# A hybrid RWKV-7 / RetNet / HGRN2 backbone on one core: the order around RWKV's score products, and who writes a token mixing's own part

## What is computed

```python
def nbr_mean_seq(p):                      # context: mean of the two neighbours in the sequence
    pp = jnp.pad(p, ((0, 0), (1, 1), (0, 0)))
    return 0.5 * (pp[:, :-2] + pp[:, 2:])

def nbr_mean_grid(p):                     # latents: mean of the four neighbours in the grid
    ...
    m = 0.25 * (g[:, :-2, 1:-1] + g[:, 2:, 1:-1] + g[:, 1:-1, :-2] + g[:, 1:-1, 2:])

def rwkv7_mixer(p, h, v_first, vres, n_ctx, mu, ...):
    shifted = jnp.concatenate([nbr_mean_seq(p[:, :n_ctx]), nbr_mean_grid(p[:, n_ctx:])], axis=1)
    p = p + mu * (shifted - p)
    r, k, v, wd_f, wd_b, ad_f, ad_b, gd = split_sizes(p, RWKV_SIZES)
    if vres is None:
        v_first = v
    else:
        v = v + (v_first - v) * jax.nn.sigmoid(v0 + (h @ v_down) @ v_up)
    ...
    # a scan over the tokens in both directions with the state
    # S = S * exp(lw) - (S kk) (a * kk)^T + v k^T,  o = S r
    bonus = (jnp.sum(r_h * dirs[0][2] * r_k_h, axis=-1, keepdims=True)
             + jnp.sum(r_h * dirs[1][2] * r_k_h, axis=-1, keepdims=True)) * v_h
```

## Time and profile before

| what | value |
|---|---|
| time, median of 3 runs | 2741.78 us (2738.88 to 3275.7) |
| the profiled execution | 2744.85 us, of it 2743.1 us from the first to the last instruction |
| busy: TensorE matmuls | 2462.0 us (90%) |
| busy: TensorE weight loads | 1856.9 us (68%) |
| busy: VectorE | 1178.4 us (43%) |
| busy: ScalarE | 923.2 us (34%) |
| busy: GpSimd | 437.1 us (16%) |
| mean granted TensorE clock | 0.943 of full speed |
| RWKV groups, layer 0 | about 249 to 760 us, 127 us each |
| RWKV groups, layer 1 | about 1777 to 2228 us, 113 us each |

### The profile page before, as it was taken

One profiled execution on the slowest core, in us unless ns is written; L12 is line 12 of the kernel. 1 busy time (PEld: TensorE's weight loads), 2 busy tenths in 40 slices (PEclk: granted clock), 3 DMA queues, 4 the chain that ended last, 5 costly groups with the idle time before them and its releaser, 6 DMA issues.

```text
span 2743.1 us, 54656 instructions
## 1 busy us (share of the span) xinstructions
PE 2462.0 (90%) x23538; PEld 1856.9 (68%) x23538; DVE 1178.4 (43%) x1831; ACT 923.2 (34%) x1308; POOL 437.1 (16%) x455
## 2 busy tenths in 40 slices
PE   4988989898999889998999989888879898898998
PEld 1553748494855568876888856466857766598998
DVE  2323444444423343445444433254453523366665
ACT  3323232223234332334223342332232334345554
POOL 0002221212123310001000000132231314400000
PEclk8999999899999989998999989999989999899999
DMA  7313322313011023332233232200000012055553
GB/s 277 126 51 117 133 73 77 115 35 147 3 62 54 35 85 96 100 123 70 92 97 95 92 125 77 71 18 25 3 24 10 18 44 73 35 177 196 157 179 103
DMA packets 64031, 239.38 MB, mean 87 GB/s; under 512 B 7088, under 2 KB 8240, under 8 KB 62512
## 3 DMA queue, kind: packets, MB, share of 16 engines
q1 hardware_dynamic: 61920, 218.13, 24.0%
q10 hardware_dynamic: 1872, 17.75, 1.6%
HBM read 230.62 MB, written 5.24 MB: 86 GB/s over the span
## 4 chain that ended last, share of the span: by engine, by line
PE 79%; DVE 8%; ACT 6%; POOL 3%; issue 2%; DMA 2%; ACTq 0%; DVEq 0%; SPq 0%; POOLq 0%
PE psum L411 13%; PE psum L384 11%; PE psum L386 11%; PE psum L385 11%; PE psum L398 10%; PE psum L758 7%; PE psum L420 2%; PE psum L762 2%; PE psum L483 2%; PE psum L720 2%; PE psum L658 1%; POOL work L1799 1%; ACT L1383 1%; PE psum L447 1%; DMA work<-in_ret_constants 1%
## 5 line engine op out<-in xcount | busy, mean ns | idle before, releaser
L398 PE MATMUL psum<-normed,weight_ring 128*128 128x512 f32 (+1 forms) x864 | 372.5, 589 | 33.4 <-ACT normed L1437 12.6
L398 PEld LDWEIGHTS psum<-normed,weight_ring 128*128 128x128 f32 x864 | 176.5, 209 | 225.8 <-issue 210.2
L411 PE MATMUL psum<-work 64*64 64x64 f32 (+1 forms) x9088 | 307.7, 222 | 14.9 <-ACT work L1618 10.5
L929 DVE TENSOR_TENSOR weight_ring_parts<-weight_ring,weights_high 128x1024 fp32r<-128x1024 f32 (+1 forms) x224 | 266.7, 1191 | 125.5 <-ACT weights_high L1398 121.1
L411 PEld LDWEIGHTS psum<-work 64*64 64x64 f32 x9088 | 294.7, 135 | 26.6 <-issue 15.6
L385 PE MATMUL psum<-normed_low_part,weights_high 128*128 128x512 f32 (+1 forms) x896 | 304.1, 339 | 0.0
L1398 ACT ACTIVATE weights_high<-weight_ring 128x1024 fp32r<-128x1024 f32 (+1 forms) x224 | 230.8, 1030 | 160.5 <-PE psum L386 149.0
L758 PE MATMUL psum<-normed,weight_ring 128*128 128x512 f32 (+1 forms) x512 | 200.6, 539 | 2.7 <-ACT work L1383 2.7
L384 PE MATMUL psum<-normed_high,weights_high 128*128 128x512 f32 (+1 forms) x512 | 178.3, 348 | 15.6 <-DVE normed_low_part L917 15.2
L385 PEld LDWEIGHTS psum<-normed_low_part,weights_high 128*128 128x128 f32 x896 | 173.3, 193 | 21.3 <-issue 0.5
L386 PE MATMUL psum<-normed_high,weight_ring_parts 128*128 128x512 f32 (+1 forms) x512 | 176.9, 346 | 0.0
(11 more groups left out here) (241 smaller groups left out, 4218.6 us busy)
## 6 DMA issues: line engine op xcount, KB each, us to landing
weight_ring<-in_weights SPq DMA_DIRECT2D x406, 512.0 KB, 3.6
x_scratch<-work ACTq DMA_DIRECT2D x2, 2048.0 KB, 7.4
weight_ring<-in_weights SPq DMA_DIRECT2D x16, 256.0 KB, 2.8
work<-x_scratch ACTq DMA_DIRECT2D x2, 2048.0 KB, 10.3
work<-in_ret_constants ACTq DMA_DIRECT2D x2, 1152.0 KB, 12.7
work<-in_small_weights ACTq DMA_DIRECT2D x2, 1152.0 KB, 5.2
work<-in_x ACTq DMA_DIRECT2D x1, 2048.0 KB, 14.8
constants<-in_constants ACTq DMA_DIRECT2D x1, 1315.0 KB, 9.1
```

Source lines behind the costliest of these rows:

```text
L398: last = mm(ps[:, 0:t1 - t0], tiled(s, k), hT[:, k, t0:t1], start=(k == 0), stop=(k == KT - 1))
L411: last = mm(ps[q, w * m:w * m + w], lhs(q, m), rhs(q, m), start=True, stop=True)
L929: tt(ring_r[:, i % RING, o], ring[:, i % RING, o], high[:, n % HIGHS, o].bitcast(F32), ALU.subtract).then_inc(vec_split.sem, vec_split.ste ...
```

## The change

Five things are done.

1. **Order of the values.** On VectorE, mixing v (now a function `values`, in layer 1 with the difference to the first layer's values) moves from ahead of the first draining of gb to behind the draining of gk of direction 0. The first level of direction 0 moves behind the draining of gb of direction 1, and the gate products (`values_gated`) behind that. On ScalarE the gate's sigmoid moves from ahead of all transposes to between direction 0's and direction 1's.
2. **Bonus.** The two bonus products become one operation, and stand behind level j = 2.
3. **Own part.** ScalarE writes (1 - mu) x of all tokens straight from PSUM into the mixing's target, as a third operation of `raw`. The bank is free only after it. VectorE's two operations for that are gone.
4. **Neighbours.** GpSimd adds only the two vertical neighbours of the grid. VectorE adds the two horizontal ones into a new scratch (`sides`), as soon as the raw copy is there, and adds both parts in separate operations, so it has three operations for the latents and one for the context.
5. **The left-over column** of the prepared keys is made by a product with one, not by a copy.

TensorE's rows are the same as before.

```diff
 def mix(i, dst, key):
-    eng.wait_ge(pool_rwkv.sem, pool_rwkv.at("neighbours", l, i))
+    eng.wait_ge(act_rwkv.sem, act_rwkv.at("raw", l, i))
...
-    if ctx:
-        ts(dst[:, 0:NC], wk(raw + 1, NC), dcol(D_OMU + i), None, ALU.mult)
-    ts(dg, grid, dcol(D_OMU + i), None, ALU.mult)
+    tt(sides.rearrange("p (r t) -> p r t", t=GRID), grid[:, 1:5, 0:64], grid[:, 1:5, 2:66], ALU.add)
+    eng.wait_ge(act_rwkv.sem, act_rwkv.at("own part", l, i))
+    stt(dst[:, NC:N], sides, dcol(D_QMU + i), dst[:, NC:N], ALU.mult, ALU.add)
+    eng.wait_ge(pool_rwkv.sem, pool_rwkv.at("neighbours", l, i))
     if ctx:
         stt(dst[:, 0:NC], wk(raw + 654, NC), dcol(D_HMU + i), dst[:, 0:NC], ALU.mult, ALU.add)
     stt(dst[:, NC:N], wk(raw + 654 + NC, NC), dcol(D_QMU + i), dst[:, NC:N], ALU.mult, ALU.add)
...
-    cp(KR3[:, :, e:e + 1], kk3[:, :, e:e + 1])
+    tt(KR3[:, :, e:e + 1], kk3[:, :, e:e + 1], over_chunks(kcol(K_ONE, 1), 1), ALU.mult)
...
-    mix(8 + c, vv, ("mixed", l, 8 + c))
...
-    ts(ks, ks, pcol(l, "rk", c), None, ALU.mult)
-    tt(ks, ks, r[:, lo:N], ALU.mult)
...
     for d in range(2):
...
+        if d == 1:
+            first_level(0)
+            if l > 0:
+                values_gated()
         eng.wait_ge(wide_filled.sem, wide_filled.at("gk", l, c, d))
...
-        tt(chunks(B + BT), chunks(B + LT), over_chunks(kcol(K_LEV, 64), 64), ALU.mult)
-        tt(chunks(B + RR), ident64(kc), chunks(B + BT), ALU.subtract)
+        if d == 0:
+            values()
+    first_level(1)
...
+        if j == 2:
+            stt(ks, ks, pcol(l, "rk", c), r[:, lo:N], ALU.mult, ALU.mult)
...
 def raw(i, dst, ps, key):
...
     act(grid, latent, ACT.Copy)
+    act(dst[:, t0:N], ps[:, 0:N - t0], ACT.Copy, scale=dcol(D_OMU + i))
...
 def neighbours(i):
...
     tt(s3, grid[:, 0:4, 1:65], grid[:, 2:6, 1:65], ALU.add)
-    tt(s3, s3, grid[:, 1:5, 0:64], ALU.add)
-    tt(s3, s3, grid[:, 1:5, 2:66], ALU.add)
```

More of the change, by code:

```diff
@@ L1538, in _ @@
                     eng.wait_ge(big_filled.sem, big_filled.at("small", l, j))
-                    raw(12 + j, big.get("small", l, j), ("drained", "small", l, j))
+                    raw(12 + j, wk(RW_SMALL + 512 * j), big.get("small", l, j), ("drained", "small", l, j))
                 if l > 0:
@@ L1585, in _ @@
                     project(2)
-                    if l > 0:
-                        eng.wait_ge(vec_rwkv.sem, vec_rwkv.at("mixed", l, 8 + c))
-                        eng.wait_ge(big_filled.sem, big_filled.at("vgate", l, c))
-                        act(wk(RW_SCR), big.get("vgate", l, c), ACT.Sigmoid, bias=pcol(l, "v0", c)).then_inc(act_rwkv.sem, act_rwkv.step(("drained", "vgate", l, c)))
-                        eng.wait_ge(act_rwkv.sem, act_rwkv.n)
-                        act_rwkv.also(("vgate sigmoid", l, c))
                     modulation("kk", l, c)
@@ L1596, in _ @@
                         for n, dst in (("tkk", chunks(B + YK, 64, 64, 128)), ("tb", chunks(B + BTT)), ("tk", chunks(B + KTT))):
+                            if l > 0 and d == 1 and n == "tkk":
+                                eng.wait_ge(vec_rwkv.sem, vec_rwkv.at("mixed", l, 8 + c))
+                                eng.wait_ge(big_filled.sem, big_filled.at("vgate", l, c))
+                                act(wk(RW_SCR), big.get("vgate", l, c), ACT.Sigmoid, bias=pcol(l, "v0", c)).then_inc(act_rwkv.sem, act_rwkv.step(("drained", "vgate", l, c)))
+                                eng.wait_ge(act_rwkv.sem, act_rwkv.n)
+                                act_rwkv.also(("vgate sigmoid", l, c))
                             eng.wait_ge(mid_filled.sem, mid_filled.at(n, l, c, d))
```

62 lines of the change are left out of this document (33 added, 29 removed).

## The result

| | before | changed |
|---|---|---|
| time, median | 2741.35 us (4 runs) | 2691.69 us (4 runs, 2690.81 to 2699.12) |
| ratio of the times | 1 | 0.9828, 95% interval 0.9805 to 0.9851 |
| span of the profiled execution | 2743.1 us | 2689.1 us |
| mean granted TensorE clock | 0.943 | 0.956 |
| busy: TensorE, VectorE, ScalarE, GpSimd | 2462.0, 1178.4, 923.2, 437.1 us | 2439.7, 1187.7, 942.7, 406.5 us |

The forecast was 2701 us; the changed kernel is 1.7% faster. The medians there were 2701.79 and 2705.62 us, with ratios of 0.9842 (0.9818 to 0.9866) and 0.9865 (0.9841 to 0.9889); one further execution, of 9735 us, is as far outside as the 3275.7 us of the first table and is left out.

A forecast was written before the change was run, and what follows sets the result against it. TensorE's matmuls were taken as the bound (79% of the chain). Layer 1's 39.5 us (4 x 9.5 + 1.5) and layer 0's 1.6 gave 41 us less: 2701 us, own bounds 2690 to 2714, widened by rivals to 2684 to 2722.

The forecast's parts named there:

- The bound, and the wait to go: TensorE's matmuls bound the kernel; in layer 1 its 31.7 us of waiting for L1170, gb's draining, would go.
- Start of a group: Layer 1, up to gb: value projection starts as before, keys are prepared earlier, gb starts 2.0 us earlier.
- From gb on: Layer 1, step by step from gb's start to the level product of direction 1, the stretch's end: 17.7 us.
- The size a group: Layer 1: stretch ends at 1931.2 instead of 1940.75, 9.5 us less in each of four groups.
- The 1.5 us expected for the first group alone: Layer 1, first group only: gain at the value projection's wait for ScalarE's draining, 2.5 us there before.
- Work costed at nothing: Sigmoid ahead of direction 1's transposes (2 us if uncovered), bonus product (0.7 if uncovered), 8-column product: each counted as zero.
- Layer 0: Layer 0: 5.3 gained from L973's wait, 2.5 ahead of groups, 4.2 lost to ScalarE, 2 to clock: 1.6 us.
- Ahead of the groups: Layer 0, wait of 3.91 us for mixing, table load and sigmoid: shorter by 1.5 plus 1.0, 2.5 us.
- A (VectorE stays the bound): Layer 1: values' mixing overlaps GpSimd's sums at up to 1.4 us; only 4.3 us a group, 2722 us; chance 0.15.
- B (the clock in layer 0): Layer 0: shorter waits keep the clock up, 3 us back in each group; 2682 us; chance 0.13.
- C (the clock falls more): All eight groups: ScalarE's third operation lengthens two waits and slows the clock, 6.9 us a group; 2750 us; chance 0.04.
- D (the values' transpose takes over the wait): Layer 1: transposing the values waits for the gate as gb did, nothing moves; 2742 us; chance 0.05.

The follow-up runs named there:

- gate_first: The changed kernel with VectorE's gate products ahead of the first level of direction 0, not behind it; 2691.04 us, ratio 0.9817.
- sigmoid_first: The changed kernel with ScalarE's gate sigmoid put back ahead of all transposes, not only those of direction 1; 2725.0 us, ratio 0.994.
- bonus_split: The changed kernel with the bonus product in its new place but as two VectorE operations again; 2695.81 us.
- order_only: The kernel before with the new VectorE and ScalarE order and the one-operation bonus inside a level, but the old mixing; 2708.35 us, ratio 0.987.
- after_again: The changed kernel unaltered, run again on another chip as yardstick; 2701.79 us, ratio 0.9842.
- after_third: The changed kernel unaltered, run again beside another later set of experiments; 2705.62 us, ratio 0.9865.
- bonus_back: The changed kernel with the two old bonus operations back at their place behind preparing the keys; 2702.61 us.
- copy_back: The changed kernel with the 8-column product made a copy again; 2695.58 us, ratio 0.982.
- own_back: The changed kernel with VectorE writing the own part again, the sum of two neighbours staying on VectorE; 2698.08 us, ratio 0.9834.

## Why the prediction was right, point by point

**The bound, and the wait to go.** Right. L1170's wait is gone but for 1.7 us, and layer 1's groups gave 42.3 us; the sum had 39.5. The prediction calls the product behind the 7.60 us gb of direction 1; it is gk of direction 0, as said above. In its own sum for the change it has the order right, so no term is wrong by it. The 0.3 us left there were to stand ahead of gb of direction 1, and 0.47 do.

**Start of a group.** L1551, ScalarE's third operation, takes 0.69 us for 128x512 as costed. The line that ends the key preparation starts 5.98 us behind the value projection. The forecast had 5.5 to 6.7 (1910.3 to 1911.5 against 1904.8), and VectorE met GpSimd's L1812 with one operation of r's mixing (1.38 us) and with the one behind it (1.37 us). gb starts 8.61 us behind the value projection, for 10.72 before: a gain of 2.1, where the sum took 2.0.

**From gb on.** The working put the end of the stretch 17.7 us behind gb; it is 17.31. The steps in between hold too: gb of direction 1 at 6.17 (6.1), gk of direction 1 behind a wait of 0.42 (0.7), the collision of a gate product with GpSimd (0.95 us more), and the transposing of the values at 13.86 (14.4). `gate_first` shows the collision's price net of what follows it: 0.75 us a group, less than the 1.3 the working had given, since the next wait in line takes back 0.84.

**The size a group.** 9.5 us were forecast for the stretch and 9.99 measured. The second group's interval shrank by 10.1 us, so nearly all of it lies in the stretch; the three intervals shrank by 10.5 on average. Of the 9.99 us, 2.8 are the clock. The 1.5 us expected for the first group alone hardly show in this execution, in which its interval shrank by 10.9 us against 10.1 and 10.4. In the kernel's other two profiled executions that interval is 99.1 and 99.2 us, 13.5 us shorter than before. The difference is the clock: the matmuls of this interval were busy for 91.95 us here, at a granted clock of 0.95, and for 87.43 us in both others, at 1.00. The first group's low-rank products had the same wait of 0.61 us for ScalarE in all three, so that wait alone does not decide it.

**Work costed at nothing.** The transposes' banks behind the sigmoid: right as the change has it. The prediction put 2 us on losing that cover, the duration of table load and sigmoid. No run takes the cover away at that place. `sigmoid_first`, which leaves the sigmoid ahead of direction 0's transposes, costs 6.0 us of waiting a group, since the sigmoid also waits until the values are mixed. So the duration alone is no measure of what a lost cover costs. The bonus product: right (`bonus_split`). The 8-column product: right, no gain. For it the prediction had cited a page of the Trainium skill (SBUF — State Buffer, "Who interferes with whom"), by which a VectorE instruction with both inputs in SBUF waits for a GpSimd instruction that reads SBUF. The trace of the changed kernel agrees, with 1.12 us for all 16 of these products. Another VectorE product of 128x8, the draining L973, which has one input in PSUM, takes 0.17 us in all 24 cases before.

**Layer 0.** Here the total of the terms was near, but not the terms. The wait for L973 (6.1 us in the earlier trace rows) is indeed gone. In its place TensorE waits longer for the weights. Waits of TensorE over layer 0's groups, before and then changed:

```profile
PE psum L447 <- DMA weight_ring<-in_weights: 14.8, 4, 4.2
PE psum L456 <- DVE derived L973: 6.1, 4, 2.6
```

```profile
PE psum L447 <- DMA weight_ring<-in_weights: 16.5, 7, 4.2
```

Waiting for both fell from 20.9 to 16.5 us, by 4.4 and not by 5.3. In the changed kernel's other executions it is 17.1 and 18.0, which leaves 3 to 4 us. The term that was too small is "the fourth set of weights lands soon after, so I leave off 0.2 a group": the three executions give 0.4 to 0.8. The cost of ScalarE's third operation came out as costed: the low-rank products wait 5.3 us for ScalarE instead of 3.1, and the projections 3.6 us for their bank instead of 1.5, 4.3 us together for the 4.2 of the sum.

Ahead of the groups the shorter chain of small mixings gave TensorE 3.1 us, not 2.5. The row at 242.78 in the earlier trace rows had 3.91 us of idle time; now (timeline, TensorE):

```profile
245.58 1.02 PE L456 MATMUL psum<-constants,work 128*128 128x2 f32 x8 [2.30 <-issue]
246.47 8.81 PE L398 MATMUL psum<-normed,weight_ring 128*128 128x512 f32 x16
```

The wait is 1.6 us shorter, less than the 2.5 forecast. Behind it the clock stays up: these eight products take 1.02 instead of 1.83 us, and the projection behind them 8.81 instead of 9.47 us. So the shorter chain was overrated by 0.9 us, and the clock behind the wait, which I had left out, gave 1.5. All variants with the new mixing have 2.3 to 2.5 us there; `order_only`, with the old mixing, has 3.90.

The first two intervals of layer 0 moved by +0.1 and -1.5 us, within the 2 us I had set. The third moved by -6.9, and how much of that is the change stays open. In `after_again` and `after_third` it was again shorter than before, by 4.5 and 6.2 us, and in all other variants but one it was 123.8 to 127.1 us. But `bonus_split`, which shares all of the change but the one bonus operation, had 130.9 us there, and the kernel before has one trace only, with 130.3. The granted clock over 511 to 641 us was 0.91 in `bonus_split` and in before, and 0.95 in the changed kernel.

The first 4.4 us of loss in the table are not explained by the change. 2.9 of them are there by the time of the wait for L883 (at 44.55 us before, 47.49 in the changed kernel), ahead of RWKV and of every line that was touched. The small projections end at 234 to 235 us in before, `order_only` and `bonus_back`, and at 237 to 240 us in all other traces. Since `bonus_back` has the new mixing and the new order, and `order_only` the new place of the bonus, no part of the change goes with it. Why that start is later I did not test.

**The rivals.** A (VectorE stays the bound): its first sign, values' mixing at 1.4 us, does not occur. B (the clock in layer 0): it occurs in part. The last two sets of modulation products of the second group took 11.92 us from the first one's start to gb before, at a granted clock of 0.57, and take 7.95 us now, at 0.79; 2.64 of these 4.0 us are the wait for L973. But the interval that holds them shrank by only 1.5 us, so the rest was lost elsewhere in the group, and 3 us a group did not come back. C (the clock falls more): the longer waits for ScalarE's third operation did come, as given above, but the granted clock over 260 to 641 us is 0.96, for 0.93 before. D (the values' transpose takes over the wait): 5.5 us out of 40.3, so no.

**The total.** 2701 us against 2691.69. Layer 1 gave 2.8 us more than its term and the small mixings 0.6 more. The rest of this execution's gain lies in layer 0's third group and in parts the change does not touch, less the 4.4 us of the later start. The kernel's later medians, 2701.79 and 2705.62, say that some 10 us of this last part are chance. That 2701 falls within 1 us of the first of them is luck, since the total holds 4.4 us of a later start that the forecast did not have.

## What to carry to other kernels

When an engine that keeps a queue in order holds up the bound engine, look at what stands between the data's arrival and the instruction that drains it, and move everything that has a later user behind it, on every engine in the chain: here VectorE's new order brought nothing that shows as long as ScalarE had not moved its sigmoid too. Count a removed wait with the slow clock behind it: 2.8 of 10 us a group here. And when work moves out of cover, price it by the whole time until it can start and end, not by its duration. Last, compare two traces by a mark on the bound engine: a mark on another engine can move with the change.

## What the runs showed of the hardware

VectorE and GpSimd seem to take turns instruction by instruction. GpSimd's two operations of L1817 started at 1891.96 and ran until 1895.53 (timeline, GpSimd, second group of layer 1):

```profile
1891.96 3.57 POOL L1817 TENSOR_TENSOR work<-work 128x512 f32<-128x512 f32 x2 [3.52 <-DVE work L1135]
...
1904.61 1.69 POOL L1831 TENSOR_TENSOR work<-work,constants 128x512 f32<-128x512 f32 x1 [7.57 <-DVE work L1170]
```

In the same time VectorE ran L1144, L1146, L1144, L1146 at 0.68, 1.12, 0.68 and 1.12 us. The large products are as fast as elsewhere (0.69 us for 512 columns), and the small ones with 8 columns take the time. That fits one reading, which I did not test apart: while a large product runs (0.68 us), GpSimd stands still, and then GpSimd works for 1.1 us while the small product waits. The 3.57 us of GpSimd's pair are 2 x 0.68 and 2 x 1.1. By that reading making the small operation cheaper cannot help, whatever its kind, as `copy_back` found, and only a different pairing in time could.

How far the clock falls behind a short wait was not the same each time. In the second group of `own_back` 1.34 us of idle time ahead of gb were followed by 1.84 us for gb and 3.40 us for the 64 transposes, for 1.56 and 2.04 in the changed kernel. In the changed kernel 1.37 us ahead of the values' transposing were followed by full speed (2.08 us for 64). The second case is in the changed kernel's timeline above, the first is here (`own_back`, TensorE):

```profile
1892.44 1.84 PE L420 MATMUL psum<-work 64*64 64x64 f32 x32 [1.34 <-DVE work L1151]
1894.03 3.40 PE L411 MATMUL psum<-constants,work 64*64 64x64 f32 x64
```
